# The order in which a two-block transformer kernel places its large buffers in SBUF

## The reference

```
for l in range(2):                       # first block
    x = x + 0.5 * swiglu(rmsnorm(x), ffn1_w_in[l], ffn1_w_out[l])     # 1024 -> 2*2816 -> 1024
    x = x + hybrid_mixer(rmsnorm(x), w_in[l], ...)                    # delta rule + stick-breaking attention
    x = x + 0.5 * swiglu(rmsnorm(x), ffn2_w_in[l], ffn2_w_out[l])
for l in range(2):                       # second block
    h = rms_norm(x)
    branches = (band attention, latent attention, forget-gate attention, causal conv)(h @ w_in[l])
    x = x + (sum over n of sigmoid(h @ w_gate[l] + b_gate)[n] * (branches[n] @ w_branch[l, n])) @ w_o[l]
    x = x + square(relu(rms_norm(x) @ w_up[l])) @ w_down[l]           # 1024 -> 4096 -> 1024
return rms_norm(x)
```

## Time and profile before

| | us |
|---|---|
| median of 3 runs | 2371.44 (2370.69 to 2371.57) |
| the profiled execution, its own time | 2372.5 |
| its span, first to last instruction | 2370.7 |
| PE busy | 2327.5 (98%) |
| DVE, ACT, POOL busy | 1587.2, 1402.8, 144.0 |
| granted TensorE clock, mean | 0.994 |

### The profile page before, as it was taken

How to read it: one execution, slowest core, us unless ns; L and a number is a source line. 1 busy time by engine, 2 the same in 40 slices (tenths; PEclk the granted TensorE clock), 3 DMA queues, 4 the chain that set the end, 5 groups by cost and what they waited for, 6 DMA issues and landing times. The chain is left out here.

```text
span 2370.7 us, 40537 instructions
## 1 busy us (share of the span) xinstructions
PE 2327.5 (98%) x17022; PEld 2191.8 (92%) x17022; DVE 1587.2 (67%) x1948; ACT 1402.8 (59%) x1874; POOL 144.0 (6%) x119
## 2 busy tenths in 40 slices
PE   8999999999999999999999999999999999999998
PEld 7999999999999999999999999889999989899997
DVE  5666668856666756667865666659785455978554
ACT  5456788555555545678745555546854454686443
POOL 0000002200000000001300000000040000004000
PEclk9999999999999999999999999999999999999999
DMA  6555444235555555544315556544455555345653
GB/s 229 195 178 179 144 142 143 72 125 178 178 199 175 190 184 188 169 143 141 126 54 177 178 171 202 177 143 125 142 178 193 194 175 163 116 152 180 202 178 124
DMA packets 312452, 385.60 MB, mean 163 GB/s; under 512 B 10812, under 2 KB 287568, under 8 KB 312272
## 3 DMA queue, kind: packets, MB, share of 16 engines
q1 hardware_dynamic: 312160, 382.96, 49.6%
q10 hardware_dynamic: 112, 0.06, 0.0%
HBM read 381.94 MB, written 1.06 MB: 162 GB/s over the span
## 5 line engine op out<-in xcount | busy, mean ns | idle before, releaser
L316 PE MATMUL bank<-xhi,whi 128*128 128x256 f32 x3696 | 1057.2, 286 | 5.0 <-DVE wlo L305 4.1
L318 PE MATMUL bank<-xhi,wlo 128*128 128x256 f32 x3696 | 1044.0, 282 | 0.0
L317 PE MATMUL bank<-xlo,whi 128*128 128x256 f32 x3696 | 1041.4, 282 | 0.0
L294 DVE TENSOR_TENSOR wlo<-raw,whi 128x2048 fp32r<-128x2048 f32 x354 | 815.8, 2306 | 188.8 <-ACT whi L278 183.7
L278 ACT ACTIVATE whi<-raw 128x2048 fp32r<-128x2048 f32 x355 | 675.8, 1905 | 203.3 <-PE bank L318 203.3
L316 PEld LDWEIGHTS bank<-xhi,whi 128*128 128x128 f32 x3696 | 702.4, 190 | 10.3 <-DVE wlo L305 4.2
L317 PEld LDWEIGHTS bank<-xlo,whi 128*128 128x128 f32 x3696 | 700.5, 190 | 5.0 <-issue 1.9
L318 PEld LDWEIGHTS bank<-xhi,wlo 128*128 128x128 f32 x3696 | 700.2, 189 | 0.0
L316 PE MATMUL bank<-whi,yhi 128*128 128x512 f32 x608 | 239.3, 394 | 0.0
L318 PE MATMUL bank<-whi,ylo 128*128 128x512 f32 x608 | 238.3, 392 | 0.0
L317 PE MATMUL bank<-wlo,yhi 128*128 128x512 f32 x608 | 237.2, 390 | 0.0
(11 more groups left out here) (397 smaller groups left out, 2904.4 us busy)
## 6 DMA issues: line engine op xcount, KB each, us to landing
raw<-in_ffn_w_in SPq DMA_DIRECT2D x88, 1024.0 KB, 5.1
raw<-in_w_in SPq DMA_DIRECT2D x88, 1024.0 KB, 5.1
raw<-in_ffn_w_out SPq DMA_DIRECT2D x44, 1024.0 KB, 4.8
raw<-in_w_gate SPq DMA_DIRECT2D x32, 1024.0 KB, 5.6
raw<-in_w_up SPq DMA_DIRECT2D x32, 1024.0 KB, 5.2
raw<-in_w_down SPq DMA_DIRECT2D x32, 1024.0 KB, 4.9
raw<-in_w_branch_b SPq DMA_DIRECT2D x8, 1024.0 KB, 4.8
raw<-in_w_branch_a SPq DMA_DIRECT2D x8, 1024.0 KB, 4.9
```

What stands on the lines that cost most here:

```text
L294: e.tensor_tensor(wlo[s][:, 0:size], raw[s][:, 0:size], whi[s][:, 0:size].bitcast(F32), ALU.subtract)\
L316: e.matmul(o, ahi, bhi, start=start, stop=False, skip_group_check=True)
L317: e.matmul(o, ahi, blo, start=False, stop=False, skip_group_check=True)
L318: return e.matmul(o, alo, bhi, start=False, stop=stop, skip_group_check=True)
```

## The change

The same buffers, with the same sizes and types, are made in another order. Every instruction of every engine is the same as before, word for word, in the same order: only the addresses behind the names differ. So there is no place at which instructions moved.

With each buffer rounded up to 32 bytes, the calls give these distances from `xhi`, in bytes modulo 512 (`x`, `xhi` and `xlo` have the same place modulo 512, before and after):

| buffer | before | after |
|---|---|---|
| whi0, wlo0 | 256, 384 | 256, 256 |
| whi1, wlo1 | 384, 0 | 96, 96 |
| whi2, wlo2 | 384, 0 | 160, 160 |
| yhi, ylo | 0, 0 | 288, 288 |
| raw0, raw1, raw2 | 128, 256, 256 | 384, 0, 0 |
| table, arena | 0, 32 | 384, 256 |

As a place in the partition, the weight slots and x lay on multiples of 128 bytes before; after, `whi1`, `wlo1`, `whi2`, `wlo2`, `yhi` and `ylo` begin 32 bytes past a multiple of 64, the others on a multiple of 128.

```diff
         room = [KC * WIDE_2, UNIT, UNIT]
-        raw = [sb(f"raw{s}", [P, room[s]]) for s in range(SLOTS)]
-        whi = [sb(f"whi{s}", [P, room[s]], F32R) for s in range(SLOTS)]
-        wlo = [sb(f"wlo{s}", [P, room[s]], F32R) for s in range(SLOTS)]
+        raw1 = sb("raw1", [P, room[1]])
+        raw2 = sb("raw2", [P, room[2]])
         x = sb("x", [P, TT, D])
         xhi = sb("xhi", [P, KC, T], F32R)
         xlo = sb("xlo", [P, KC, T], F32R)
+        gate_bias = sb("gate_bias", [P, DEPTH * 32])
+        whi0 = sb("whi0", [P, room[0]], F32R)
+        raw0 = sb("raw0", [P, room[0]])
+        conv_w = sb("conv_w", [P, DEPTH * 96])
+        wlo0 = sb("wlo0", [P, room[0]], F32R)
+        table = sb("table", [P, CONSTANTS.shape[1]])
+        b_forget = sb("b_forget", [P, DEPTH * 4])
+        dt_bias = sb("dt_bias", [P, DEPTH * HEADS])
+        whi1 = sb("whi1", [P, room[1]], F32R)
+        wlo1 = sb("wlo1", [P, room[1]], F32R)
+        a_log = sb("a_log", [P, DEPTH * HEADS])
+        whi2 = sb("whi2", [P, room[2]], F32R)
+        wlo2 = sb("wlo2", [P, room[2]], F32R)
+        pre = [sb(f"pre{i}", [P, 2, T + 3]) for i in range(2)]
+        const_cols = sb("const_cols", [P, 4])
+        sumsq = sb("sumsq", [P, 4])
         yhi = sb("yhi", [P, KC, T], F32R)
         ylo = sb("ylo", [P, KC, T], F32R)
-        table = sb("table", [P, CONSTANTS.shape[1]])
+        later_keys = sb("later_keys", [P, 384])
+        raw, whi, wlo = [raw0, raw1, raw2], [whi0, whi1, whi2], [wlo0, wlo1, wlo2]
```

More of the change, by code:

```diff
@@ L136, in hybrid_stack_kernel @@
         ident, ones, le, ge = const("ident"), const("ones"), const("le"), const("ge")
-        const_cols = sb("const_cols", [P, 4])
         eps, one, ln_scale, half_pi = [const_cols[:, i:i + 1] for i in range(4)]
@@ L140, in hybrid_stack_kernel @@
         cols = sb("cols", [P, NV])
[L141 to L144, removed]
         lnv = sb("lnv", [P, TT])
@@ L147, in hybrid_stack_kernel @@
         arena = sb("arena", [P, ARENA])
-        gate_bias = sb("gate_bias", [P, DEPTH * 32])
         dw = sb("dw", [P, DEPTH * 62])
-        b_forget = sb("b_forget", [P, DEPTH * 4])
         rotary = sb("rotary", [96, 2 * T])
@@ L164, in hybrid_stack_kernel @@
         conv_rows = arena[0:96, 4352:4608].rearrange("p (l n) -> p l n", l=DEPTH)
-        pre = [sb(f"pre{i}", [P, 2, T + 3]) for i in range(2)]
         small = sb("small", [P, 240])
-        later_keys = sb("later_keys", [P, 384])
         xn = arena[:, 0:TT * D].rearrange("p (t d) -> p t d", t=TT)
```

## The result

The changed kernel takes 2381.65 us (median; 2380.82 to 2383.35), the kernel before in the same comparison 2370.83 (2370.59 to 2371.57). The ratio is 1.0043, with a 95% interval of 1.0032 to 1.0053: slower by 0.43%, where 2357 was forecast. The span of the profiled execution went from 2370.7 to 2379.6 us, at a mean granted clock of 0.995 against 0.994.

A forecast was written before the change was run, and what follows sets the result against it. PE was taken to be the bound, by the start-to-start time of its float32r matmuls. 14.9 us gained less 1.1 lost gave 13.8 off the 2370.7 span, 2356.9 (2357.6 off the median); range 2310 to 2386.

The forecast's parts named there:

- What bounds the kernel: PE, busy 98% of the span: 15,024 float32r matmuls one after another, at their start-to-start time, with nothing feeding PE late.
- its last doubt: A buffer start 32 bytes past a multiple of 64 might count by itself, making the 292-column units a poor guide; unsized.
- 7 ns: Large products, at 118.3 ns a matmul, lose some 7 ns against arena's 128-column matmuls at 111.3 ns.
- the third rival: "The collisions vanish": matmuls of slots 1 and 2 fall to 111.3 ns, 2318.6 us; chance 0.13.
- The 1.6 ns a matmul: Gain for each of 9312 matmuls whose distance leaves the multiples of 128: 14.9 us (4.7 to 19.6).
- Slot 0 "nothing, at most 1.3 us": Slot 0 against x, 4416 matmuls: wlo from 384 to 256 changes nothing, at most 1.3 us.
- the sign of wrong working: Slot 0's units moving by more than 0.03 us, or the difference sitting in waits, would show the forecast's working wrong.
- y: Products with y off multiples of 128 gain 1.6 ns each; slot 2's 384 with y stationary lose 1.1 us.
- Distance 0 is what pays: First rival: wlo at 0 in slots 1 and 2 is the good case; 12.1 us lost, 2383.5 us; chance 0.25.
- No change: Second rival: two reads at once may cost the 7 ns wherever they are; 2371.4 us within 3; chance 0.20.
- The collisions vanish: At 96 and 160 the reads may never meet; slots 1 and 2 gain 52.8 us, 2318.6 us; chance 0.13.

The follow-up runs named there:

- The map: Mean start-to-start spacings by distance modulo 256, collected from all kernels with whi and wlo at one distance: 113.8 to 120.0 ns with weights stationary, 227.8 to 234.6 with 512 columns.
- The unlike pairs: Changed kernel with whi at 64 in every slot, wlo at 0, 192 and 224, y at 0: 2361.18 us in a single run.

## Why the prediction was wrong

*What bounds the kernel: right.* PE's starts carry the change, at a mean granted clock of 0.994 and 0.995, and the waits answer for 3 us of it by the busy times, for under 1 us counted by starts. The unit times were the rows to look at. That a start 32 bytes past a multiple of 64 might count by itself, its last doubt, can be dropped: with the distances kept and all places shifted, the time stayed (ratio 1.0005).

Two readings on the way were wrong. In the earlier trace rows the load takes 0.19 us from 1330.07, so by the trace it isn't through when L318's stream begins at 1330.19; the rows show that the two overlap and not what starts the stream. And the 24 that the earlier trace rows counts are 12 matmuls: the kernel issues 32 matmuls at L1472, all float32, and the trace has 64 records for them, two each. The 111.3 ns are half of such a matmul of 128 columns, no measure for a float32r matmul of 256, so the "7 ns" lost against it had no ground. The sum didn't use it; the third rival did.

*The 1.6 ns a matmul: this step failed.* I took it from the 272-column chunks, in which the weights move and x is stationary, and gave it to 6672 matmuls in which the weights are stationary. The map shows that the two forms don't share their good and bad places: 0 is the best distance with 512 weight columns moving and, beside 160, the worst with weights stationary. And I made one class of all distances that are no multiples of 128. They differ among each other by more than the classes: 113.5 at the best, 120.0 at 160, on which the change put the slot with the second most matmuls. In place of 4176 x 1.6 = 6.7 us gained, slot 2 lost 4176 x 1.66 = 6.9. Slot 1 gained 0.3 ns of the 1.6.

The odd chunks of the earlier trace rows are at 64 and 192 modulo 256, never at 96 or 160. Over both 272-column units of the trace the difference holds, at 126.6 for even and 124.3 ns for odd chunks, so the reading was not the fault. That row could not speak for the change's distances, whatever the form. The 292-column chunks did pass them, among many other distances, and a mean over 21 starts can't tell one of these from the rest.

*Slot 0 "nothing, at most 1.3 us": wrong.* `wlo` from 384 to 256 cost 0.65 ns x 4416 = 2.9 us. I had priced one of three lines with a third of the difference between slots. The unlike pairs show why that fails: the spacing belongs to the pair, not to a sum over lines. The row printed above moved by 0.02 us a unit, under the 0.03 that I had named as the sign of wrong working; the mean over all units is 0.65 x 48 = 31 ns.

*y: right in sign in part.* With y moving, slots 0 and 1 gained 2.2 and 4.4 ns instead of 1.6, while slot 2 at 384 lost 0.9. With y stationary slot 1, at 320, gained 0.5 only, slot 0 lost some 2 and slot 2 3.1 (I had 2.9 for it). Together 0.8 us gained where the 1.6 gave some 3.4 less 1.1. The kernel with y at 0 shows that, with the weight slots where the change puts them, y's new place is worth about 5 us, nearly all in slot 1 (384 x 3.6 ns + 1200 x 3.7 ns = 5.8): without it the change would have lost more.

*The rivals.* "Distance 0 is what pays" gave 2383.5, near the 2381.65 measured, and its point of decision (slot 2 over 5.68 us) was met. It had the time by luck, for a wrong reason: a slot at distance 0 takes 119.9 ns. Slots 1 and 2 were quicker before because their pair was (384, 0). It also wanted 232.9 ns for slot 1's row products, and they stayed at 229.2, since y was at 320 from them. "No change" is refuted by the interval (1.0032 to 1.0053) and by all that follows from distance alone: 2329.87 to 2386.94 us with the same instructions. What the traces show is that the mean spacing of these matmuls, each beside a load, lies between 113.5 and 120.0 ns by where the two operands lie. The Trainium skill, on the page TensorE: Matmul & The Clock Gate, in its section Step-by-step: what each phase is for, has the next weights' load take no read bandwidth from the running matmul; for these float32r matmuls, with a load for each, the measurement speaks against the reading that addresses are therefore free. Where in the chip the two operands meet, no run here shows. "The collisions vanish" was nearer to the truth than its chance: there are distances at which 113.5 ns is reached in all slots, though not its 111.3. 96 and 160 just aren't among them.

What stays open: what in the hardware makes the period of 256 bytes and why the good place ends within 8 bytes, and what picks one of the two even spacings when both weights are at 64.

## What to carry to other kernels

Where PE runs matmul after matmul, each with its own weight load, read the time from start to start by buffer and by form: if the same shape runs at different spacings in different buffers, the distance between the two operands is a knob that costs no instruction, and here it was worth 1.7% (0.9828). Measure a map for the form that has the counts and never take it from another form or from a mean over distances. Of two places with the same best spacing take the one at which every unit keeps it, and look at single units, since a mean can hide two kinds of them.

## What the runs showed of the hardware

Three things I had not expected. The spacing of 128x128x256 float32r matmuls depends on (weights less x) modulo 256 bytes, with means between 113.5 and 120.0 ns, and not on the place itself (all moved by 32 bytes: ratio 1.0005); 8 bytes beside the best distance it is back at 117.9. It belongs to the pair of loads: 64 with 192 gives 114.0, 64 with 0 gives 118.5 on the mean. And where both loads are at 64 a unit runs at one of two even spacings, 113.5 or 118.0, and in the first block's feed-forward passes keeps one of them after the first units. The runs of the kernel with 320 and 64 mixed spread from 2346.03 to 2354.2 us; how much of that is the two spacings isn't shown, since one run alone has a trace and the granted clock went with the time (0.996 in the quickest, 0.992 in the slowest).
